# Decoder layer on one core: smaller last weight pieces, and a normalization step on GpSimd

## The chip, the cores and the metric

The kernel runs on one NeuronCore of a Trainium2 chip. The metric is the device time of one execution in microseconds, the median of several runs. A profile is one further execution; its span is the time from the first to the last event recorded on the core.

## The reference

One layer of a decoder trunk over 256 tokens of width 1024, all in float32. Two attention groups, a cross-attention and a mixture of 32 experts follow each other, each with a residual and a layer norm. The part that matters here is the last:

```python
def moe_ffn(h, w_router, b_router, w_mlp1, b_mlp1, w_mlp2, b_mlp2):
    ...
    y = jnp.zeros_like(xt)
    for e in range(N_EXPERTS):
        hid = clamped_swiglu(xt @ w_mlp1[e] + b_mlp1[e])
        y = y + combine[:, e:e + 1] * (hid @ w_mlp2[e] + b_mlp2[e])
    return y.reshape(B, S, D)
...
        ffn = moe_ffn(h, w_router[l], b_router[l], w_mlp1[l], b_mlp1[l], w_mlp2[l], b_mlp2[l])
        h = layer_norm(DEEPNORM_ALPHA * h + ffn, ln3_g[l], ln3_b[l])
```

Every token goes to 4 of the 32 experts. An expert has an up matrix of 1024 x 2048 (8 MB) and a down matrix of 1024 x 1024 (4 MB).

## The kernel before

**Stages.** The attention part takes the first fifth. Then the experts run one after another. For one expert TensorE gathers its up to 64 tokens (`gather`, L969), multiplies them with the up matrix (`up_stage`, L1059: 8 chunks `k` of 128 rows, 1 MB each, four products of 128x512 a chunk), VectorE and ScalarE form the clamped SwiGLU, TensorE turns it (`turn_hidden`, L1018) and multiplies with the down matrix (`down_stage`, L1097: two halves `u` of four chunks `c`, 0.5 MB and two products each), ScalarE copies the result (L1405), and TensorE scatters it into four banks (`scatter`, L981), which hold the sum for all tokens: banks 4 and 5 the two halves of the first 128 tokens, banks 6 and 7 those of the other 128. A product is two MATMUL instructions in the trace. Each expert's down stage runs behind the next expert's up stage, so that the order at the end is: up of 31, down of 30, down of 31, last scatter, final norm.

**Weights.** `ring` in SBUF has 24 places of 1 MB: two sets (parity) of two up pieces and one down piece, 4 MB each. SyncE issues all loads on one queue and waits ahead of each for the place to be free (`up_used`, `up_done`, `down_used`, `down_done`). In the loop a piece is one transfer. The last experts load halves of 2 MB, and the down pieces of experts 30 and 31 quarters of 1 MB (`load_quarter`, L558), each with a semaphore of its own: for the last, `last_half_in[0]`, `first_half_in`, `last_half_in[1]`, `piece_in`. TensorE waits for them ahead of chunk 0 and 2 of each half. The last expert's up piece comes in halves: chunks 6 and 7 wait for one transfer. Between the halves of the last down stage TensorE does the scatter of expert 30.

**Final norm.** The first 128 tokens: VectorE takes statistics from banks 4 and 5 (L1490 to L1494), GpSimd raises the variance to the power -0.5 (L599), and VectorE does two steps for each half of 512 columns: `(x - mean) * gain` out of the bank (L1500), then `x * rstd + bias` (L1504). The other 128: ScalarE sums (L1431) and sums squares (L1438) out of banks 6 and 7, GpSimd takes the power (L609), VectorE does the same two steps (L1911, L1914). ScalarE's passes write their elementwise output, which nobody reads, into `result[:, 1]`. SyncE sends each half to `out` as 256 KB (L580), when the semaphore `ln_ready` counts it, and waits for all four. The order on each engine is the order of the code.

## Time and profile before

| | us |
|---|---|
| median of 3 runs | 1140.28 |
| lowest and highest run | 1139.02, 1140.31 |
| the profiled execution | 1139.08 |
| its span | 1137.2 |
| TensorE matmul busy | 1090.2 (96%) |
| VectorE busy | 320.8 (28%) |
| ScalarE busy | 225.0 (20%) |
| GpSimd busy | 9.1 (1%) |

The span is 1.88 us shorter than the profiled execution's own time; the rest lies around it. TensorE's share is that of rows with pipelined ends. Times within the trace count from the span's start. The expert stage runs from about 230 us to 1128, the final norm from there to the end.

### The profile page before, as it was taken

What the parts mean: (1) busy time and instruction counts of PE and PEld (TensorE: products, weight loads), DVE (VectorE), ACT (ScalarE), POOL (GpSimd) and SP (SyncE); (2) the same over time, 40 slices, a digit from 0 to 9 for tenths busy, and PEclk for the clock granted to TensorE, in tenths of its full rate; (3) what the DMA queues carried; (4) which work ended last, traced back from release to release, by engine and by line L of the source; (5) the groups of instructions that cost most, each with busy time, mean ns of one, the idle gap of its engine ahead of it and who ended that gap; (6) DMA issues with size and microseconds to landing.
All of it is one profiled execution on the core that took longest, in us unless ns stands there. A gap on an engine that the chain in (4) does not pass through costs nothing.

```text
span 1137.2 us, 15690 instructions
## 1 busy us (share of the span) xinstructions
PE 1090.2 (96%) x6527; PEld 522.5 (46%) x6528; DVE 320.8 (28%) x727; ACT 225.0 (20%) x406; POOL 9.1 (1%) x14
## 2 busy tenths in 40 slices
PE   9999999999999999999999999999999999999996
PEld 6888899844333333334333333333333333334321
DVE  6987775552111111112111111111111111012113
ACT  5667565331000001001001000000000000001001
POOL 0000000000000000000000000000000000000000
PEclk9999999989999999999999999999999999999998
DMA  9856866699999999999999999999999999999996
GB/s 354 299 187 246 288 205 252 243 415 430 435 434 429 436 426 440 426 440 426 440 426 440 425 441 425 441 425 441 425 441 425 441 425 441 425 432 430 429 428 249
DMA packets 40144, 446.73 MB, mean 393 GB/s; under 512 B 4528, under 2 KB 5424, under 8 KB 24272
## 3 DMA queue, kind: packets, MB, share of 16 engines
q1 hardware_dynamic: 39824, 445.75, 93.5%
q10 hardware_dynamic: 288, 0.52, 0.1%
q8 instruction: 24, 0.39, 0.1%
q14 instruction: 8, 0.07, 0.0%
HBM read 445.21 MB, written 1.05 MB: 392 GB/s over the span
## 4 chain that ended last, share of the span: by engine, by line
PE 57%; DMA 38%; DVE 2%; SPq 1%; issue 1%; ACT 0%; DVEq 0%
DMA ring<-in_w_mlp 36%; PE bank L1059 24%; PE bank L1097 9%; PE bank L632 4%; PE bank L634 4%; PE bank L633 4%; PE bank L981 4%; PE bank L969 2%; DMA sub_g<-in_diff_subln_g 1%; PE bank L1018 1%; DMA w_raw<-in_w_in 1%; PE bank L873 1%; PE bank L857 1%; PE bank L1033 1%; SPq L465 0%
## 5 line engine op out<-in xcount | busy, mean ns | idle before, releaser
L1059 PE MATMUL bank<-ring,live 128*64 128x512 f32 x2048 | 471.2, 608 | 26.4 <-DMA ring<-in_w_mlp 25.8
L1059 PEld LDWEIGHTS bank<-ring,live 128*64 128x64 f32 x2048 | 144.2, 139 | 310.6 <-issue 290.8
L1097 PE MATMUL bank<-ring,live 128*64 128x512 f32 x992 | 220.4, 595 | 4.9 <-DMA ring<-in_w_mlp 4.9
L1796 DVE COPY live<-bank 128x256 f32<-128x256 f32 x32 | 13.6, 424 | 525.4 <-PE bank L1011 525.4
L1097 PEld LDWEIGHTS bank<-ring,live 128*64 128x64 f32 x992 | 68.7, 137 | 130.4 <-issue 122.0
L1401 ACT ACTIVATE live<-bank 128x512 f32<-128x512 f32 x31 | 18.5, 597 | 323.5 <-PE bank L1018 323.5
L1880 DVE TENSOR_SCALAR live<-bank 128x256 f32<-128x256 f32 x64 | 24.2, 420 | 199.0 <-PE bank L1059 199.0
L1473 DVE TENSOR_TENSOR w_low<-w_raw,w_high 128x1024 fp32r<-128x1024 f32 x61 | 72.0, 1222 | 14.5 <-ACT w_high L1186 14.2
L1397 ACT ACTIVATE live<-live 128x512 f32<-128x512 f32 x32 | 20.4, 636 | 246.2 <-DVE live L1880 246.2
L1186 ACT ACTIVATE w_high<-w_raw 128x1024 fp32r<-128x1024 f32 x61 | 62.8, 1059 | 28.6 <-DMA w_raw<-in_w_in 13.4
L969 PEld LDWEIGHTS bank<-pick,live 128*128 128x128 bf16 x1488 | 52.0, 118 | 25.2 <-issue 25.2
L632 PE MATMUL bank<-w_high,left 128*128 128x512 f32 x158 | 62.7, 397 | 0.5 <-DVE w_low L1473 0.2
L981 PE MATMUL bank<-live 64*128 64x512 f32 x248 | 61.6, 615 | 0.3 <-ACT live L1405 0.3
L634 PE MATMUL bank<-w_low,left 128*128 128x512 f32 x158 | 61.6, 390 | 0.0
L633 PE MATMUL bank<-w_high,left 128*128 128x512 f32 x158 | 61.6, 390 | 0.0
L1405 ACT ACTIVATE live<-bank 128x512 f32<-128x512 f32 x31 | 18.5, 597 | 203.6 <-PE bank L1097 203.6
L969 PE MATMUL bank<-pick,live 128*128 128x64 bf16 x1488 | 55.3, 198 | 0.0
L981 PEld LDWEIGHTS bank<-live 64*128 64x128 f32 x248 | 21.3, 186 | 41.0 <-issue 40.2
L632 PEld LDWEIGHTS bank<-w_high,left 128*128 128x128 f32 x158 | 29.7, 188 | 7.8 <-DVE w_low L1473 0.8
L634 PEld LDWEIGHTS bank<-w_low,left 128*128 128x128 f32 x158 | 29.6, 188 | 6.3
L633 PEld LDWEIGHTS bank<-w_high,left 128*128 128x128 f32 x158 | 29.7, 188 | 5.9
L1018 PEld LDWEIGHTS bank<-const,live 128*128 128x128 f32 x128 | 17.9, 210 | 26.0 <-issue 26.0
(233 smaller groups left out, 805.1 us busy)
## 6 DMA issues: line engine op xcount, KB each, us to landing
ring<-in_w_mlp SPq DMA_DIRECT2D x73, 4096.0 KB, 46.9
ring<-in_w_mlp SPq DMA_DIRECT2D x42, 2048.0 KB, 48.1
w_raw<-in_w_in SPq DMA_DIRECT2D x21, 512.0 KB, 8.8
w_raw<-in_w_mem_kv SPq DMA_DIRECT2D x16, 512.0 KB, 4.6
ring<-in_w_mlp SPq DMA_DIRECT2D x8, 1024.0 KB, 37.6
w_raw<-in_w_mix_out SPq DMA_DIRECT2D x8, 512.0 KB, 5.2
w_raw<-in_w_mem_q SPq DMA_DIRECT2D x8, 512.0 KB, 3.8
w_raw<-in_w_mem_o SPq DMA_DIRECT2D x8, 512.0 KB, 4.2
```

Of the source, the lines that this page charges most:

```text
L632: pe.matmul(out, stationary[0], moving[0], start=start, stop=False)
L633: pe.matmul(out, stationary[1], moving[0], start=False, stop=False)
L634: return pe.matmul(out, stationary[0], moving[1], start=False, stop=stop)
L969: mm = pe.matmul(xg[:, SLOTS * c:SLOTS * (c + 1)], h_parts[:, t, part, at:at + 4 * P - 3:4], pick[:, t, :], start=(n == 0), stop=(n == 5))
L981: mm = pe.matmul(acc[t][g][:, :], weights[rows, t, :], rows_out[rows, :], start=first, stop=last)
L1018: mm = pe.transpose(to[:, P * q:P * (q + 1)], glu[:, q:512:4], ident)
L1059: mm = pe.matmul(up[j][64 * g:64 * g + SLOTS, :], x_e[:, k, :], columns(row, j, g), start=False, stop=(k == KC - 1))
L1097: mm = pe.matmul(to[64 * g:64 * g + SLOTS, :], stationary[:, P * c + 64 * u:P * c + 64 * u + SLOTS], slot(at)[:, col:col + 512], start=(u ...
L1186: act.activation(w_high[:, (u + 2) % SPLIT], w_raw[:, u % RAW], ACT.Copy).then_inc(high_ready, 1)
L1397: act.activation(sig, glu, ACT.Sigmoid, scale=SW_ALPHA).then_inc(sig_ready, 1)
L1473: dve.tensor_tensor(w_low[:, u % RAW], w_raw[:, u % RAW], w_high[:, (u + 2) % SPLIT].bitcast(F32), ALU.subtract).then_inc(low_ready, 1)
L1880: last = dve.tensor_scalar(glu[:, S * n:S * (n + 1)], hid[:, :, 0], LIMIT, None, ALU.min)
```

## The change

**Pieces.** The second half of the last expert's second up piece is loaded as two transfers of 1 MB, and TensorE waits for each ahead of chunks 6 and 7 (`last_up_in`, then `piece_in`). Of the last down piece the first and the last quarter are loaded as two eighths of 0.5 MB each; TensorE waits for them ahead of chunks 0, 1 and 6, 7. That makes three more transfers (one up, two down).

**Norm.** VectorE centres both halves of the first 128 tokens, `(x - mean) * gain`, and counts them in `last_centred`. GpSimd then multiplies with `rstd` and adds the bias, as two instructions for each half (`stretch_last`): the first half ahead of the power for the other 128 tokens, the second behind it. VectorE centres both halves of the other 128 tokens, each behind a wait for ScalarE's sum of squares of that half, and then does both second steps. ScalarE's elementwise outputs go to `unused_out`, a place of the ring that is no longer needed. The outputs of the first 128 tokens wait for `first_out`, those of the others for `ln_ready`.

```diff
@@ -247,6 +247,7 @@
         last_y = at_place("last_y", [P, 512], F32, 4, 2048)
         last_back = at_place("last_back", [P, NT, P], F32, 4, 4096)
         result = at_place("result", [P, NT, D], F32, 1)
+        unused_out = at_place("unused_out", [P, 2, 512], F32, 6)
         mean_parts, square_sums = stats[:, 1, 0, 0:3], stats[:, 1, 1, 0:3]
 
         filled_to = {}
@@ -473,14 +477,23 @@
                         sp.wait_ge(up_used, before * 3 + 2)
                     load(e, k, 3 * parity + k)
 
-            def load_up_halves(e, before, parity):
+            def load_part(e, k, at, of, count, landed):
+
+                part = slice(8192 * of // count, 8192 * (of + 1) // count)
+                sp.dma_start(slot(at)[:, part], expert_src(e, k)[:, part]).then_inc(landed, 16)
+
+            def load_up_halves(e, before, parity, last=False):
 
                 for n in range(2 * UPS):
                     if n < 3:
                         sp.wait_ge(up_used, before * 3 + n + 1)
                     else:
                         sp.wait_ge(up_done, before + 1)
-                    load_half(e, n // 2, 3 * parity + n // 2, n % 2)
+                    if last and n == 3:
+                        load_part(e, 1, 3 * parity + 1, 2, 4, last_up_in)
+                        load_part(e, 1, 3 * parity + 1, 3, 4, piece_in[3 * parity + 1])
+                    else:
+                        load_half(e, n // 2, 3 * parity + n // 2, n % 2)
 
             def load_down(e, before, parity):
 
@@ -557,7 +570,7 @@
                 part = slice(2048 * quarter, 2048 * (quarter + 1))
                 sp.dma_start(slot(at)[:, part], expert_src(e, UPS)[:, part]).then_inc(landed, 16)
 
-            load_up_halves(E - 1, sp.snap(more * E + (E - 3)), 1)
+            load_up_halves(E - 1, sp.snap(more * E + (E - 3)), 1, last=True)
             sp.wait_ge(down_used, sp.snap(more * E + (E - 3)))
             load_quarter(E - 2, UPS, 0, before_last_half_in[0])
             load_quarter(E - 2, UPS, 1, first_half_in[UPS])
@@ -565,20 +578,24 @@
             load_quarter(E - 2, UPS, 2, before_last_half_in[1])
             load_quarter(E - 2, UPS, 3, piece_in[UPS])
             sp.wait_ge(down_used, sp.snap(more * E + (E - 2)))
-            load_quarter(E - 1, 3 + UPS, 0, last_half_in[0])
+            load_part(E - 1, UPS, 3 + UPS, 0, 8, last_eighth_in[0])
+            load_part(E - 1, UPS, 3 + UPS, 1, 8, last_half_in[0])
             load_quarter(E - 1, 3 + UPS, 1, first_half_in[3 + UPS])
             sp.wait_ge(down_done, sp.snap(more * E + (E - 2)))
             load_quarter(E - 1, 3 + UPS, 2, last_half_in[1])
-            load_quarter(E - 1, 3 + UPS, 3, piece_in[3 + UPS])
+            load_part(E - 1, UPS, 3 + UPS, 6, 8, last_eighth_in[1])
+            load_part(E - 1, UPS, 3 + UPS, 7, 8, piece_in[3 + UPS])
 
             sp.wait_ge(up_done, sp.snap(sweeps * E))
             for i, name in enumerate(("ln3_g", "ln3_b")):
                 sp.dma_start(last_gb[:, i, :], row(a[name])).then_inc(last_gb_in, 16)
-            for t in range(NT):
-                for q in range(2):
-                    sp.wait_ge(ln_ready, 12 + 2 * t + q + 1)
-                    sp.dma_start(a["out"][0, P * t:P * (t + 1), 512 * q:512 * (q + 1)],
-                                 result[:, t, 512 * q:512 * (q + 1)]).then_inc(out_written, 16)
+            for t, q in ((0, 0), (0, 1), (1, 0), (1, 1)):
+                if t:
+                    sp.wait_ge(ln_ready, 12 + q + 1)
+                else:
+                    sp.wait_ge(first_out, q + 1)
+                sp.dma_start(a["out"][0, P * t:P * (t + 1), 512 * q:512 * (q + 1)],
+                             result[:, t, 512 * q:512 * (q + 1)]).then_inc(out_written, 16)
             sp.wait_ge(out_written, 16 * 2 * NT)
 
 
@@ -605,8 +622,19 @@
             pool.tensor_tensor(rms[:, 2, :], rms[:, 1, :], half.broadcast_to([P, 8]), ALU.pow).then_inc(rms_rstd, 1)
             for n in range(2, 7):
                 inverse_root(n)
+
+            def stretch_last(q):
+                x = result[:, 0, 512 * q:512 * (q + 1)]
+                pool.wait_ge(last_centred, q + 1)
+                pool.wait_ge(rstd_ready, 7)
+                pool.tensor_scalar(x, x, ln_s[:, 6, 1:2], None, ALU.mult).then_inc(last_scaled, 1)
+                pool.wait_ge(last_scaled, q + 1)
+                pool.tensor_tensor(x, x, last_gb[:, 1, 512 * q:512 * (q + 1)], ALU.add).then_inc(first_out, 1)
+
+            stretch_last(0)
             pool.wait_ge(last_var_ready, 1)
             pool.tensor_tensor(ln_s[:, 7, 1:2], ln_s[:, 7, 0:1], half, ALU.pow).then_inc(rstd_ready, 1)
+            stretch_last(1)
 
 
         @block.tensor
@@ -1022,7 +1050,7 @@
 
                 return rows[:, 1024 * j:1024 * (j + 1)].rearrange("p (m a n) -> p m a n", a=2, n=8)[:, :, g, :]
 
-            def up_stage(n, at, loads, first_loads=None, earlier=None, first=False, first_sum=False, weights=False, bias=False, tokens=False, scatter_first=False):
+            def up_stage(n, at, loads, first_loads=None, earlier=None, first=False, first_sum=False, weights=False, bias=False, tokens=False, scatter_first=False, seventh=None):
 
 
 
@@ -1049,8 +1077,12 @@
                 for k in range(KC):
                     if k % 4 == 0 and first_loads:
                         pe.wait_ge(first_half_in[at + k // 4], first_loads)
-                    if k % 4 == (2 if first_loads else 0):
+                    if k == KC - 2 and seventh is not None:
+                        pe.wait_ge(seventh, 16)
+                    elif k % 4 == (2 if first_loads else 0):
                         pe.wait_ge(piece_in[at + k // 4], loads)
+                    if k == KC - 1 and seventh is not None:
+                        pe.wait_ge(piece_in[at + 1], loads)
                     if first and k == 4:
                         pe.wait_ge(x_e_ready, 1)
                     for j in range(2):
@@ -1079,15 +1111,17 @@
                 pe.wait_ge(back_ready, n)
                 gather()
 
-            def down_stage(n, at, loads, to, first_loads=None, stationary=hidT, between=None, halves=(None, None)):
+            def down_stage(n, at, loads, to, first_loads=None, stationary=hidT, between=None, halves=(None, None), eighths=None):
 
 
                 pe.wait_ge(hidT_ready, n)
                 for u in range(2):
                     for c in range(4):
-                        if c == 0 and halves[u] is not None:
+                        if eighths is not None and 4 * u + c in (0, KC - 2):
+                            pe.wait_ge(eighths[u], 16)
+                        if c == (1 if eighths is not None and u == 0 else 0) and halves[u] is not None:
                             pe.wait_ge(halves[u], 16)
-                        if c == (0 if halves[u] is None else 2):
+                        if c == (0 if halves[u] is None else 3 if eighths is not None and u else 2):
                             if first_loads and u == 0:
                                 pe.wait_ge(first_half_in[at], first_loads)
                             else:
@@ -1138,7 +1172,7 @@
             up_stage(of_end[1], ups[0], loads, 64, earlier=(of_end[3], of_end[2]))
             gather_next(of_end[1])
             down_stage(of_end[2], downs[1], pe.snap(loads - 16), ty, 48)
-            up_stage(of_end[0], ups[1], loads, 64, earlier=(of_end[2], of_end[1]), scatter_first=True)
+            up_stage(of_end[0], ups[1], loads, 64, earlier=(of_end[2], of_end[1]), scatter_first=True, seventh=last_up_in)
             pe.wait_ge(back_ready, of_end[0])
             turn_picks(of_end[0])
             down_stage(of_end[1], downs[0], loads, ty, 48, between=lambda: turn_hidden(of_end[0], up[0]),
@@ -1149,7 +1183,8 @@
                 pe.wait_ge(back_ready, of_end[0])
                 scatter()
 
-            down_stage(of_end[0], downs[1], loads, up[1], 64, last_hidT, between=scatter_before, halves=last_half_in)
+            down_stage(of_end[0], downs[1], loads, up[1], 64, last_hidT, between=scatter_before, halves=last_half_in,
+                       eighths=last_eighth_in)
             pe.wait_ge(y_ready, of_end[0])
             pe.wait_ge(back_ready, pe.snap(more * E + (E + 1)))
             scatter(last=True)
@@ -1428,14 +1463,14 @@
             copy_result(end, banks[1][:, :], last_y[:, :])
             for q in range(2):
                 act.wait_ge(all_added, 2 + q + 1)
-                act.activation(result[:, 1, 512 * q:512 * (q + 1)], banks[6 + q][:, :], ACT.Copy, scale=-1.0 / D,
+                act.activation(unused_out[:, q, :], banks[6 + q][:, :], ACT.Copy, scale=-1.0 / D,
                                accum_out=mean_parts[:, q:q + 1]).then_inc(tail_sums, 1)
             act.wait_ge(tail_sums, 2)
             act.activation(mean_parts[:, 2:3], mean_parts[:, 0:1], ACT.Identity, bias=mean_parts[:, 1:2])\
                 .then_inc(minus_mean_ready, 1)
             act.wait_ge(minus_mean_ready, 1)
             for q in range(2):
-                act.activation(result[:, 1, 512 * q:512 * (q + 1)], banks[6 + q][:, :], ACT.Square, bias=mean_parts[:, 2:3],
+                act.activation(unused_out[:, q, :], banks[6 + q][:, :], ACT.Square, bias=mean_parts[:, 2:3],
                                accum_out=square_sums[:, q:q + 1]).then_inc(tail_sums, 1)
                 if q == 0:
                     act.wait_ge(tail_sums, 3)
@@ -1903,13 +1938,19 @@
             step(last)
             variance(6)
             dve.wait_ge(last_gb_in, 32)
-            apply_norm(6, result[:, 0, :], [banks[4 + q][:, :] for q in range(2)], last_gb)
-            dve.wait_ge(minus_mean_ready, 1)
-            dve.wait_ge(last_var_ready, 1)
             for q in range(2):
                 half_row = slice(512 * q, 512 * (q + 1))
-                step(dve.scalar_tensor_tensor(out=result[:, 1, half_row], in0=banks[6 + q][:, :], scalar=mean_parts[:, 2:3],
-                                              in1=last_gb[:, 0, half_row], op0=ALU.add, op1=ALU.mult))
+                dve.scalar_tensor_tensor(out=result[:, 0, half_row], in0=banks[4 + q][:, :], scalar=mv_ln[:, 6, 0:1],
+                                         in1=last_gb[:, 0, half_row], op0=ALU.subtract, op1=ALU.mult).then_inc(last_centred, 1)
+            dve.wait_ge(minus_mean_ready, 1)
+            for q in range(2):
+                half_row = slice(512 * q, 512 * (q + 1))
+                dve.wait_ge(tail_sums, 3 + 2 * q)
+                dve.scalar_tensor_tensor(out=result[:, 1, half_row], in0=banks[6 + q][:, :], scalar=mean_parts[:, 2:3],
+                                         in1=last_gb[:, 0, half_row], op0=ALU.add, op1=ALU.mult).then_inc(second_mean, 1)
+            for q in range(2):
+                half_row = slice(512 * q, 512 * (q + 1))
+                dve.wait_ge(second_mean, q + 1)
                 dve.wait_ge(rstd_ready, 8)
                 dve.scalar_tensor_tensor(out=result[:, 1, half_row], in0=result[:, 1, half_row], scalar=ln_s[:, 7, 1:2],
                                          in1=last_gb[:, 1, half_row], op0=ALU.mult, op1=ALU.add).then_inc(ln_ready, 1)
```

How the instructions stand on the engines (the tag in brackets is the semaphore waited for). TensorE in the last down stage (`last_hidT` is the last expert's hidden product), before:

```order
L1097 MATMUL bank<-ring,last_hidT 64x512 [waits last_half_in0,hidT_ready]
L1097 MATMUL bank<-ring,last_hidT 64x512 x3
L1097 MATMUL bank<-ring,last_hidT 64x512 [waits first_half_in5]
L1097 MATMUL bank<-ring,last_hidT 64x512 x3
L981 MATMUL bank<-live 128x512 [waits back_ready,y_ready]
L981 MATMUL bank<-live 128x512 x3
L1097 MATMUL bank<-ring,last_hidT 64x512 [waits last_half_in1]
L1097 MATMUL bank<-ring,last_hidT 64x512 x3
L1097 MATMUL bank<-ring,last_hidT 64x512 [waits piece_in5]
L1097 MATMUL bank<-ring,last_hidT 64x512 x3
```

and after:

```order
L1131 MATMUL bank<-ring,last_hidT 64x512 [waits last_eighth_in0,hidT_ready]
L1131 MATMUL bank<-ring,last_hidT 64x512
L1131 MATMUL bank<-ring,last_hidT 64x512 [waits last_half_in0]
L1131 MATMUL bank<-ring,last_hidT 64x512
L1131 MATMUL bank<-ring,last_hidT 64x512 [waits first_half_in5]
L1131 MATMUL bank<-ring,last_hidT 64x512 x3
L1009 MATMUL bank<-live 128x512 [waits back_ready,y_ready]
L1009 MATMUL bank<-live 128x512 x3
L1131 MATMUL bank<-ring,last_hidT 64x512 [waits last_half_in1]
L1131 MATMUL bank<-ring,last_hidT 64x512 x3
L1131 MATMUL bank<-ring,last_hidT 64x512 [waits last_eighth_in1]
L1131 MATMUL bank<-ring,last_hidT 64x512
```

The last pair waits for `piece_in5`. No product has moved; two waits are added, and the scatter stays between the halves.

VectorE's final norm behind the variance, before (`last_gb` holds gain and bias, `stats` the mean of the other 128 tokens, `ln_s` the powers):

```order
L1500 SCALAR_TENSOR_TENSOR result<-bank,mv_ln,last_gb 128x512 [waits last_gb_in]
L1504 SCALAR_TENSOR_TENSOR result<-result,ln_s,last_gb 128x512 [waits rstd_ready,dve_step]
L1500 SCALAR_TENSOR_TENSOR result<-bank,mv_ln,last_gb 128x512
L1504 SCALAR_TENSOR_TENSOR result<-result,ln_s,last_gb 128x512 [waits dve_step]
L1911 SCALAR_TENSOR_TENSOR result<-bank,stats,last_gb 128x512 [waits last_var_ready,minus_mean_ready]
L1914 SCALAR_TENSOR_TENSOR result<-result,ln_s,last_gb 128x512 [waits rstd_ready,dve_step]
L1911 SCALAR_TENSOR_TENSOR result<-bank,stats,last_gb 128x512
L1914 SCALAR_TENSOR_TENSOR result<-result,ln_s,last_gb 128x512 [waits rstd_ready,dve_step]
```

and after:

```order
L1943 SCALAR_TENSOR_TENSOR result<-bank,mv_ln,last_gb 128x512 [waits last_gb_in]
L1943 SCALAR_TENSOR_TENSOR result<-bank,mv_ln,last_gb 128x512
L1949 SCALAR_TENSOR_TENSOR result<-bank,stats,last_gb 128x512 [waits tail_sums,minus_mean_ready]
L1949 SCALAR_TENSOR_TENSOR result<-bank,stats,last_gb 128x512 [waits tail_sums]
L1955 SCALAR_TENSOR_TENSOR result<-result,ln_s,last_gb 128x512 [waits rstd_ready,second_mean] x2
```

Two of the eight instructions have left the engine, and GpSimd, which before had only the powers, has this in its last rows:

```order
L616 TENSOR_TENSOR ln_s<-ln_s,small 128x1 [waits var_ready] x5
L630 TENSOR_SCALAR result<-result,ln_s 128x512 [waits rstd_ready,last_centred]
L632 TENSOR_TENSOR result<-result,last_gb 128x512 [waits last_scaled]
L636 TENSOR_TENSOR ln_s<-ln_s,small 128x1 [waits last_var_ready]
L630 TENSOR_SCALAR result<-result,ln_s 128x512 [waits rstd_ready,last_centred]
L632 TENSOR_TENSOR result<-result,last_gb 128x512 [waits last_scaled]
```

The second power (L636) now stands behind the first multiply and add.

## Rows read from the trace of the kernel before

**Rows 1.** The page's 40 slices of the span: GB/s that the DMA engines moved.
```profile
GB/s 354 299 187 246 288 205 252 243 415 430 435 434 429 436 426 440 426 440 426 440 426 440 425 441 425 441 425 441 425 441 425 441 425 441 425 432 430 429 428 249
```
**Rows 2.** The chain of waits, its end: start us, us, what.
```profile
1083.32 34.49 DMA ring<-in_w_mlp
...
1117.85 1.94 PE bank L1097 x8
...
1134.05 0.75 DVE result L1914
```
**Rows 3.** Timeline of PE and its weight loads: start us, us, instruction, idle before.
```profile
1103.18 3.65 PE L1059 MATMUL bank<-ring,live 128*64 128x512 f32 x16 [1.25 <-DMA ring<-in_w_mlp]
...
1112.99 0.32 PEld L1097 LDWEIGHTS bank<-ring,live 128*64 128x64 f32 x4 [0.54 <-DMA ring<-in_w_mlp]
1115.52 1.94 PE L1097 MATMUL bank<-ring,last_hidT 128*64 128x512 f32 x8 [0.47 <-DMA ring<-in_w_mlp]
...
1121.64 3.65 PE L1097 MATMUL bank<-ring,last_hidT 128*64 128x512 f32 x16
```
**Rows 4.** Line L558, last expert: its first two quarters, then its last two.
```profile
L558 SPq DMA_DIRECT2D ring<-in_w_mlp x2: 328/381/434, 1082.9 to 1083.3; - x2
...
DMA to landing us min/median/max: 32.4/33.5/34.5
...
L558 SPq DMA_DIRECT2D ring<-in_w_mlp x2: 4214/5456/6699, 1087.4 to 1094.2; - x2
...
DMA to landing us min/median/max: 28.6/30.7/32.8
```
**Rows 5.** DMA view of the first 28 us: GB/s in 40 slices, packets.
```profile
GB/s 0 0 47 126 277 258 234 291 281 354 404 401 407 410 401 406 399 400 423 424 421 421 395 410 404 404 415 424 433 410 430 383 407 416 402 402 422 383 395 404
DMA packets 4943, 9.89 MB, mean 353 GB/s; under 512 B 412, under 2 KB 924, under 8 KB 4942
```
**Rows 6.** Timeline of the final norm: VectorE (DVE), GpSimd (POOL), ScalarE (ACT).
```profile
1128.79 0.15 DVE L1494 TENSOR_SCALAR ln_s<-mv_ln 128x1 f32<-128x1 f32 x1
1128.86 0.74 DVE L1500 SCALAR_TENSOR_TENSOR result<-bank,mv_ln,last_gb 128x512 f32<-128x512 f32 x1
1129.02 0.55 POOL L599 TENSOR_TENSOR ln_s<-ln_s,small 128x1 f32<-128x1 f32 x1 [898.40 <-DVE ln_s L1494]
1129.68 0.75 DVE L1504 SCALAR_TENSOR_TENSOR result<-result,ln_s,last_gb 128x512 f32<-128x512 f32 x1
...
1130.29 0.19 ACT L1438 ACTIVATION_READ_ACCUMULATOR result<-bank,stats 128x1 f32 x1
1130.35 0.74 DVE L1500 SCALAR_TENSOR_TENSOR result<-bank,mv_ln,last_gb 128x512 f32<-128x512 f32 x1
...
1131.19 0.19 ACT L1438 ACTIVATION_READ_ACCUMULATOR result<-bank,stats 128x1 f32 x1
...
1131.79 0.55 POOL L609 TENSOR_TENSOR ln_s<-ln_s,small 128x1 f32<-128x1 f32 x1 [2.21 <-ACT ln_s L1445]
```
**Rows 7.** Timeline, GpSimd's earlier powers and what VectorE ran beside them.
```profile
19.76 2.35 DVE L1473 TENSOR_TENSOR w_low<-w_raw,w_high 128x1024 fp32r<-128x1024 f32 x2
19.92 1.46 POOL L599 TENSOR_TENSOR ln_s<-ln_s,small 128x1 f32<-128x1 f32 x1 [1.00 <-DVE ln_s L1494]
...
97.07 1.65 POOL L605 TENSOR_TENSOR turned_weights<-turned_weights,small 128x8 f32<-128x8 f32 x1 [75.69 <-DVE turned_weights L1713]
...
137.03 0.74 DVE L1500 SCALAR_TENSOR_TENSOR h<-h,mv_ln,gb 128x512 f32<-128x512 f32 x1
137.20 0.98 POOL L599 TENSOR_TENSOR ln_s<-ln_s,small 128x1 f32<-128x1 f32 x1 [38.48 <-DVE ln_s L1494]
```
**Rows 8.** Line L580, outputs; then a stretch's busy times, PEclk, DMA share, GB/s.
```profile
L580 SPq DMA_DIRECT2D out<-result x4: 332/334/343, 1130.5 to 1134.8; - x4
...
DMA to landing us min/median/max: 2.0/2.0/2.0
...
1130.30:1132.40 2.10, 0.00 (x0) 0.00 (x0) 2.06 (x4) 1.34 (x6) 0.55 (x1) 0.50 0.32 125
```

3 lines of the change are left out of this document (added).

## Prediction

> **What bounds the kernel now.** I read the slices of the page first, then the chain of waits, then the timeline of the last 40 us engine by engine. The slices [rows 1] show 415 to 441 GB/s from the ninth to the last but one, with no gap: from there on the kernel takes expert weights as fast as they come. The chain [rows 2] says the same of the end: one stretch of weight transfer runs up to 1117.81, and only behind it do compute engines set the time. So an edit counts only if it makes the second quarter of the last down piece land earlier, or shortens what follows: TensorE from 1117.85 to 1125.3, the copy and last scatter to 1128.05, the final norm on VectorE to 1134.80, the last output transfer and the end at 1137.2. What has room ahead of 1117.85 is no gain unless it moves that landing.
>
> **Part 1: smaller pieces.** What TensorE does with them, step by step.
> *Last up piece.* Before, chunks 6 and 7 of the last expert wait for one 2 MB transfer; TensorE idles 1.25 us in front of 1103.18 and then runs both in 3.65 us, to 1106.83 [rows 3]. Now chunk 6 waits for its own 1 MB. It lands about 2.4 us earlier (1.05 MB at 430 GB/s, [rows 1]), near 1100.8, while TensorE is still busy until 1103.18 - 1.25 = 1101.93. So the 1.25 us go and the up stage ends near 1105.6. What is late next: the down stage of expert 30, whose four quarters arrive about 2.4 us apart, each with 8 MATMULs, half of 3.65, so 1.83 us of work. It ends 0.47 ahead of 1115.52 now, at 1115.05 [rows 3]; by the same arrivals it would end no earlier than 1112.99, where the weight loads wait for the fourth quarter [rows 3], plus 1.83, which is 1114.8. Of the 1.25 us some 0.2 is left, and the next wait takes that: the last down stage starts at 1115.52 for its first quarter, and its third and fourth chunks at 1117.85 for the second [rows 2, 3].
> *First eighths.* Chunk 0 can start near 1114.8 rather than 1115.5, but chunks 2 and 3 still wait for the second quarter, issued at 1083.3 and landed 34.5 us later, at 1117.8 [rows 4]. The bytes ahead of it in the queue are the same. Gain 0.
> *Last eighths.* The fourth quarter was issued at 1094.2 and landed 28.6 us later, at 1122.8 [rows 4]. TensorE starts the second half of that stage at 1121.64 and comes to chunk 6 after 8 of its 16 instructions, 1121.64 + 1.83 = 1123.47 [rows 3]. The data has been there for 0.67 us. Gain 0, as long as that cover lasts; if the fourth quarter came over 0.67 us later, the eighths would save at most the rest, up to 0.9 us.
> *Cost.* Three more transfers are issued on SyncE, at 0.33 to 0.43 us where the queue takes them at once [rows 4], with over 28 us of queue behind: nothing. The eighths move 4 KB rows. The nearest rows for small packets are the first 28 us, where all but one are under 8 KB: once full, the slices there move 383 to 433 GB/s [rows 5], about 405, against 430. For the 1.05 MB of eighths ahead of the second quarter that is 2.59 - 2.44 = 0.15 us at worst, at best 0. The quarters of 8 KB rows landed 2.4 us apart, so they cost nothing. I take 0. The gains of ScalarE and VectorE (hidden product 1.25 us earlier) end in the same waits. The two rows of the last gain and bias are issued when the up stage is done, 1.2 us earlier, behind all weights in the queue.
> **Part 1 is worth 0**, from -0.9 to +0.15.
>
> **Part 2: the final norm.** Before, VectorE runs eight instructions of 0.74 to 0.75 us behind the variance, from 1128.86 to 1134.80 [rows 2, 6]. Now two of them, the second steps of the first 128 tokens, go to GpSimd as four: multiply and add for each half, in line with the two powers. VectorE keeps six. Centring both halves has no wait in between, start 0.67 apart as other rows do: 1128.86 to 1130.27. The centring of the other 128 tokens waits for ScalarE's first sum of squares, 1130.48, and the second, 1131.38 [rows 6]: 1130.56 to 1131.30 and 1131.46 to 1132.2. The last two steps wait for the power, which ended at 1132.34 [rows 6]. If GpSimd cost nothing VectorE would end at 1132.45 + 0.67 + 0.75 = 1133.87, 0.93 earlier. But the outputs now leave in the order (0,0), (0,1), (1,0), (1,1) on one queue, and (0,1) comes from GpSimd's last add, so both later ones stand behind it.
>
> *GpSimd's price.* It has no row of 128x512. From below: VectorE's 0.75 for the same shape [rows 6], so 1.50 a pair. From above: its power of 8 elements took 1.65, of one 0.55 [rows 7], 0.157 per element; at that rate a half row takes 80 us. A power is far from a multiply, and I give that end no more than a few in a hundred and leave it outside the range. Between them I add to VectorE's 0.75 what GpSimd's one-element row costs above VectorE's of 0.15 (L1494 [rows 6]), 0.40: 1.15 for the add with two inputs. For the multiply with one input I take 0.95. Pair: 2.10; for the range up to 3.0, twice VectorE's rows.
> [...]
>
> *The queue.* Power of token half 0 to 1129.57; multiply from 1129.68 (the first centring ends 1129.60) to 1130.63; 0.10 for the wait; add to 1131.88. The second power stands behind that: it starts at 1131.91, not 1131.79. So 0.12 is lost there, and it ends at 1132.46. Then multiply and add of the second half.
>
> *The port.* The earlier powers [rows 7] show what happens when the two engines meet. A power of one element takes 0.55 beside a VectorE row that reads a bank (1129.02 [rows 6]). Beside an instruction with two inputs in SBUF it takes as long as that lasts and 0.41 to 0.45 more: started 137.20, the other ended 137.77, it ended 138.18; started 19.92, the other (1.18 each) ended 20.93, it ended 21.38. So only one of them has the interface, and it is given back between two VectorE instructions. The last steps on VectorE have both inputs in SBUF. I take it that it holds both ways. GpSimd's second multiply starts right behind its own power, 1132.49 to 1133.44; VectorE, which needs 0.11 to hear of the power, stands behind it: 1133.44 to 1134.14. Then GpSimd's add, 1134.14 to 1135.29, and VectorE's last step, to 1135.99.
> The Trainium skill, SBUF — State Buffer, section "SBUF: two separate sides", states this as an exclusive lock held for the whole instruction, by a VectorE instruction with two SBUF inputs against a GpSimd one that reads SBUF, whoever starts first. The powers [rows 7] agree with it in one direction; the other no run here shows yet.
>
> *The outputs.* A 256 KB output lands 2.0 us after its issue, issues take 0.34, and one keeps the DMA engines 0.32 x 2.1 = 0.67 us [rows 8]. Before they were 1.1 us and more apart. Now three go in a row: issues at 1135.34, 1135.68, 1136.03. The third lands at 1136.03 + 2.0 at the earliest, but the three transfers need 1135.34 + 1.33 + 3 x 0.67 = 1138.67. Before, the last landed at 1134.83 + 2.0 = 1136.83, 0.37 before the end. **Part 2 costs** 1138.67 + 0.37 - 1137.2 = 1.84, say 1.9 us.
>
> **Sum.** The profiled execution took 1139.08, 1.88 more than its span, and lies 1.20 under the median of 1140.28. I put 1.9 on the median: 1142.2.
>
> **Rivals.**
> *A, no blocking* (the port is shared when GpSimd comes first). Then add at 1133.54 to 1134.69, issue 1134.74, landed 1138.07, end 1138.44: +1.2, 1141.5. For it: no row of before has GpSimd ahead of VectorE. Against: the three stretched powers.
> *C, VectorE first at the port*, which ends on the slower side. Both start within 0.1 us of the power's end. If VectorE gets in first: step 1132.57 to 1133.32, multiply to 1134.27, last step to 1134.97, add to 1136.12, three issues from 1136.17, end 1139.87: +2.7, 1143.0, 0.24% above before. It decides from the point where GpSimd takes more than 0.1 us from its power to its next read. For it: after the port came free the power took 0.41 of its 0.55, so some 0.14 lies ahead of its read.
> *D, GpSimd dearer than 2.3 us a pair.* Each 0.1 us on a pair counts twice, once before the second power, once behind. At 2.5 case B (the forecast) gives +2.7, at 3.0 it gives +3.7, 1144.0.
> *E, cheap GpSimd or late weights.* At 1.5 a pair, without blocking and with outputs that overlap in the DMA engines, the last issue is at 1134.7, -0.1; in executions where the fourth quarter comes late, the eighths take back up to 0.9. 1139.4 to 1140.7. For it: the runs of before spread over 1.3 us, and the profile is one of the fast ones.
> *F, the pieces don't do what they say*: the second quarter is the wait that counts and stays whole. That is in the forecast already.
>
> **How the numbers follow.** About 0.2% (2.3 us) is what a measurement of this kernel can tell from no change. Forecast 0.33, A 0.24, C 0.15, D 0.12, E 0.16. Range: from 1139.8, inside E, to 1144.0, the upper end of D. Slower by over 0.2% is above 1142.6: C 0.12, D 0.12 and 0.08 of the forecast's own spread, 0.32. Faster is below 1138.0, deep in E: 0.04. The rest, 0.64, is the same.
>
> **What would show it.** Right: TensorE's last up rows without the 1.25 us gap, and the third chunk of the last down stage still at about 1117.8; GpSimd's multiply and add near 0.95 and 1.15; VectorE's first last step twice as long as 0.75 or late; the second power near 1131.9; three outputs issued 0.34 apart, the last landing more than 2.0 after its issue. Wrong: a landing of the second quarter that moves by over 0.3 us, a multiply or add over 1.3, VectorE's last steps of 0.75 beside a GpSimd row (then A), or an end of VectorE before 1134.

## The result, and the profile after

The changed kernel takes 1143.21 us in the median of its runs, against 1140.31 for the kernel before: a ratio of 1.0025, 95% interval 1.0017 to 1.0033, or 2.9 us slower. Its profiled execution took 1141.85, with a span of 1140.1 (before 1139.08 and 1137.2). Of eleven executions of each kernel one was far off, at 2222.55 before and 4011.12 after, and the ratio leaves both out. The result is inside the range of the prediction and 1.0 us above the point; at 0.25% slower it lies beyond the 0.2% to which the prediction drew "the same".

TensorE behind the last up stage, from the timeline of the changed kernel (start us, us, instruction, idle before it and what ended it):

```profile
1098.28 7.09 PE L1091 MATMUL bank<-ring,live 128*64 128x512 f32 x32 [0.23 <-DMA ring<-in_w_mlp]
...
1105.73 1.94 PE L1131 MATMUL bank<-ring,live 128*64 128x512 f32 x8
1108.08 1.94 PE L1131 MATMUL bank<-ring,live 128*64 128x512 f32 x8 [0.41 <-DMA ring<-in_w_mlp]
...
1114.80 1.89 PE L1131 MATMUL bank<-ring,last_hidT 128*64 128x512 f32 x8
...
1118.00 1.94 PE L1131 MATMUL bank<-ring,last_hidT 128*64 128x512 f32 x8 [1.31 <-DMA ring<-in_w_mlp]
...
1126.21 1.99 PE L1009 MATMUL bank<-last_y,last_back 64*128 64x512 f32 x8 [0.77 <-ACT last_y L1440]
```

The same third chunk in the timeline of the kernel before:

```profile
1117.85 1.94 PE L1097 MATMUL bank<-ring,last_hidT 128*64 128x512 f32 x8 [0.39 <-DMA ring<-in_w_mlp]
```

The gap of 1.25 us inside the last up stage [rows 3] is gone: 32 instructions run in one piece. Two waits for weights take its place: 0.41 us in expert 30's down stage, which had none there, and in front of the third chunk of the last down stage 1.31 us instead of 0.39. That chunk starts at 1118.00, 0.15 later than before. From there to the last scatter it is 8.21 us in both.

The final norm, same view, VectorE (DVE), GpSimd (POOL) and SyncE's queue:

```profile
1129.01 1.40 DVE L1943 SCALAR_TENSOR_TENSOR result<-bank,mv_ln,last_gb 128x512 f32<-128x512 f32 x2
...
1129.90 1.57 POOL L630 TENSOR_SCALAR result<-result,ln_s 128x512 f32<-128x512 f32 x1 [0.18 <-DVE result L1943]
...
1130.73 1.58 DVE L1949 SCALAR_TENSOR_TENSOR result<-bank,stats,last_gb 128x512 f32<-128x512 f32 x2 [0.32 <-ACT unused_out L1473]
...
1131.56 1.27 POOL L632 TENSOR_TENSOR result<-result,last_gb 128x512 f32<-128x512 f32 x1
1132.78 0.57 POOL L636 TENSOR_TENSOR ln_s<-ln_s,small 128x1 f32<-128x1 f32 x1
1132.85 4.84 SPq L597 DMA_DIRECT2D out<-result  x4
1133.34 1.57 POOL L630 TENSOR_SCALAR result<-result,ln_s 128x512 f32<-128x512 f32 x1
1133.46 1.77 DVE L1955 SCALAR_TENSOR_TENSOR result<-result,ln_s,last_gb 128x512 f32<-128x512 f32 x2 [1.15 <-POOL ln_s L636]
1134.99 1.36 POOL L632 TENSOR_TENSOR result<-result,last_gb 128x512 f32<-128x512 f32 x1
```

VectorE's two last steps by line (count: duration ns min/median/max, first and last start us; shapes):

```profile
L1955 DVE SCALAR_TENSOR_TENSOR result<-result,ln_s,last_gb x2: 737/924/1111, 1133.5 to 1134.5; 128x512 f32<-128x512 f32 x2
```

GpSimd's multiply takes 1.57 us, its add 1.27 and 1.36. The second power starts at 1132.78 instead of 1131.79 [rows 6]. VectorE ends at 1135.23, GpSimd at 1136.35, where VectorE alone ended at 1134.80. The outputs, by the line of their issues, from 1136.7 on (the third and fourth):

```profile
L597 SPq DMA_DIRECT2D out<-result x2: 431/446/461, 1136.8 to 1137.2; - x2
...
DMA to landing us min/median/max: 2.3/2.3/2.4
```

The last one is issued at 1137.2 instead of 1134.8, and lands 2.4 us later instead of 2.0 [rows 8].

**How the traces are compared.** The weights run up to 3 us earlier or later from one execution to the next, long before anything that was changed. So each trace is read in three stretches: W, from chunk 4 of the last up stage to the third chunk of the last down stage (the weights); T, from there to the last scatter (TensorE); N, from there to the span's end (the norm). The spans are given to 0.1 us, so an N is good to 0.05 and a difference of two to 0.1. e4, e5, e6, e8, e9 and e10 ran once each, for their traces.

| kernel | W | T | N |
|---|---|---|---|
| before | 19.58 | 8.21 | 11.14 |
| changed | 19.72 | 8.21 | 13.89 |
| e1, pieces alone | 19.72 | 8.21 | 11.16 |
| e2, norm alone | 19.53 | 8.21 | 13.86 |
| e3, other order of outputs | 19.72 | 8.21 | 12.53 |
| e4, multiply with two inputs | 19.71 | 8.21 | 12.94 |
| e5, last steps from the bank | 19.67 | 8.21 | 13.76 |
| e6, one half on GpSimd | 19.58 | 9.03 | 11.78 |
| e7, VectorE alone | 19.48 | 8.21 | 10.60 |
| e8, up quarters only | 19.58 | 8.21 | 11.19 |
| e9, eighths only | 19.62 | 8.21 | 11.15 |
| e10, multiply by a constant | 19.57 | 8.21 | 13.71 |

N grew by 2.75 us, W by 0.14. That is the 2.9. (In e11 and e12 the scatter has moved, so they have no W and T of this kind and stand below.)

### The profile page after: what moved, and what is told of

It reads as the page before. It is cut to its first block, busy times and chain, and to the rows that moved or that the text cites. A ratio compares the mean times of both kernels' runs of the same rounds, so it can differ in the third digit from the quotient of the medians.

```text
span 1140.1 us, 15697 instructions
## 1 busy us (share of the span) xinstructions
PE 1089.1 (96%) x6528; PEld 524.0 (46%) x6528; DVE 319.5 (28%) x725; ACT 225.2 (20%) x406; POOL 14.9 (1%) x18
## 4 chain that ended last, share of the span: by engine, by line
PE 57%; DMA 37%; SPq 2%; DVE 1%; issue 0%; ACT 0%; POOL 0%; POOLq 0%; another core or an unknown queue 0%
DMA ring<-in_w_mlp 36%; PE bank L1091 23%; PE bank L1131 9%; PE bank L660 5%; PE bank L662 5%; PE bank L661 5%; PE bank L1009 4%; PE bank L997 2%; DMA w_raw<-in_w_in 2%; SPq L483 1%; PE bank L1046 1%; PE bank L901 1%; PE bank L885 1%; SPq L469 1%; PE bank L1061 1%
## 5 line engine op out<-in xcount | busy, mean ns | idle before, releaser
L1091 PE MATMUL bank<-ring,live 128*64 128x512 f32 x2048 | 470.1, 607 | 24.4 <-DMA ring<-in_w_mlp 23.8
```

The costliest lines, as they stand in the source:

```text
L1091: mm = pe.matmul(up[j][64 * g:64 * g + SLOTS, :], x_e[:, k, :], columns(row, j, g), start=False, stop=(k == KC - 1))
```

## The experiments

My theory behind the trace: all but 0.15 us is GpSimd's, by the length of its four instructions, by the place of the second power behind two of them, and by outputs that stand behind its last add. The rivals: the pieces slow the weights; the new order of VectorE's steps loses by itself; GpSimd is slow only because the port is contended.

### The two parts apart (e1, e2)

e1 is the diff without its norm hunks, e2 the diff without its piece hunks.

> The change's first part alone: the last up piece in quarters and the eighths, with the final norm of the kernel before. My theory (the pieces move no landing that counts, all of the loss is GpSimd's) expects 0.0 us against the kernel before, 0.3 at most, with the third chunk of the last down stage near 1117.9 us and an idle gap of some 1.3 us ahead of it. The rival (smaller packets or fewer bytes in the queue slow the weights) expects the 0.14 us by which that chunk was later in the changed kernel, or more in executions other than the profiled one: up to 1.5 of the 2.9 us here.

> The change's second part alone: the norm step on GpSimd, with the weight pieces of the kernel before. My theory expects the whole loss, +2.7 to +2.9 us, with GpSimd's multiply at 1.57 us and its add at 1.27 to 1.36, the second power at about 1132.6, and the last issue of an output near 1137.1. The rival expects 1.4 to 2.5.

e1 measured 1140.63 in the median against 1140.43, ratio 1.0006 (0.9997 to 1.0015); e2 1142.74, ratio 1.0019 (1.0010 to 1.0028). These repeated runs alone leave the pieces between -0.3 and +1.7 us. They put e2 2.3 us above the kernel before (1.1 to 3.2), less than the 2.7 to 2.9 expected and inside the rival's 1.4 to 2.5, so they do not decide between the two. The stretches are sharper. e1 has N = 11.16, as before, and W = 19.72; e2 has all of the loss in N, 13.86, and W = 19.53. The timeline of e1 shows the gap in front of the third chunk, with the norm as it was:

```profile
1114.13 1.89 PE L1117 MATMUL bank<-ring,last_hidT 128*64 128x512 f32 x8
1117.33 1.94 PE L1117 MATMUL bank<-ring,last_hidT 128*64 128x512 f32 x8 [1.31 <-DMA ring<-in_w_mlp]
```

So the loss in N is the norm's, and what the pieces gained in the up stage ended in this wait.

### Which of the pieces costs (e8, e9)

e8 keeps the two quarters of the last up half and drops the eighths; e9 the reverse.

> Only the last up half in two transfers, nothing else of the change. From the start of chunk 4 of the last expert's up stage to that of the third chunk of its last down stage it took 19.58 us before and 19.72 with all pieces. If the 4 KB rows of the eighths cost that, 19.58 here, and TensorE runs its last 32 up instructions without the gap of 1.25 us; if it is the number of transfers or the up quarters, 19.65 to 19.72.

> Only the eighths of the last down piece, with the last up half whole. If the 4 KB rows cost the 0.14 us, the stretch from chunk 4 of the last up stage to the third chunk of the last down stage takes 19.72 us here; otherwise 19.6. The 1.2 us gap in front of the last 16 up instructions is back. The stretch from that third chunk to the last scatter stays 8.21 us, with or without eighths.

W was 19.58 in e8 and 19.62 in e9. The six traces with all pieces (changed, e1, e3, e4, e5, e10) have 19.57 to 19.72, mean 19.69, the four with the pieces of before (before, e2, e6, e7) 19.48 to 19.58, mean 19.54. The pieces cost about 0.14 us together. Which of them, and whether it is the rows of 4 KB or the number of transfers, stays open: e8 came out as it should if the 4 KB rows cost it, but e9, which has them, came out at 19.6 as it should if they do not, and both lie within the spread of the others.

### The order of the outputs (e3)

```diff
-            for t, q in ((0, 0), (0, 1), (1, 0), (1, 1)):
+            for t, q in ((0, 0), (1, 0), (1, 1), (0, 1)):
```

> The changed kernel with one edit: the outputs leave in the order (0,0), (1,0), (1,1), (0,1), so that the two of VectorE do not stand behind GpSimd's last one. Theory: in the changed kernel the last three issues were bunched behind the end of the last add (1136.35), and the last one landed 2.4 us after its issue instead of 2.0. With this order the last issue is at 1136.4 and lands at 1138.4: 1.1 to 1.3 us less than the changed kernel, so +1.7 us against before. If the end of GpSimd's work alone set the time and the transfers overlapped, it would be 0 to 0.4 us less.

e3 measured 1141.67 in the median, ratio 1.0010 (1.0001 to 1.0019), 1.2 us above the kernel before where 1.7 was expected. N fell by 1.36 us to 12.53. The last output left right behind GpSimd's add, which ended at 1138.61, and landed 2.0 us later. The add in the timeline of e3

```profile
1137.25 1.36 POOL L632 TENSOR_TENSOR result<-result,last_gb 128x512 f32<-128x512 f32 x1
```

and by line of the issue:

```profile
L597 SPq DMA_DIRECT2D out<-result x1: 332/332/332, 1138.6 to 1138.6; - x1
...
DMA to landing us min/median/max: 2.0/2.0/2.0
```

So about half of the loss in N was outputs queued behind the slowest one: two issues (0.8 us), 0.4 of landing in a bunch, and some 0.1 between the last landing and the end.

### What GpSimd's multiply costs (e4, e10)

e4 reads the deviation as a row of equal elements, e10 multiplies by a constant:

```diff
-                pool.tensor_scalar(x, x, ln_s[:, 6, 1:2], None, ALU.mult)
+                pool.tensor_tensor(x, x, ln_s[:, 6, 1:2].broadcast_to([P, 512]), ALU.mult)
```

```diff
-                pool.tensor_scalar(x, x, ln_s[:, 6, 1:2], None, ALU.mult)
+                pool.tensor_scalar(x, x, 0.5, None, ALU.mult)
```

> The changed kernel with GpSimd's multiply as an instruction with two tensor inputs (the reciprocal deviation read as a row of 512 equal elements) instead of one with a scalar. If GpSimd's time goes with the number of inputs, it takes as long as the multiply or longer, 1.57 us or more. If the form with a scalar is the slow one, it takes 1.27 us as the add, and the pair 2.54 instead of 2.84; as each pair stands once before and once behind the second power, the end moves by 0.6 us.

> The changed kernel with GpSimd's multiply by the constant 0.5 in the instruction instead of the column of reciprocal deviations, so that the first 128 tokens are not scaled by their own. The multiply took 1.57 us with the column and 1.04 us as a two-input instruction. If the column operand makes it slow, it takes 1.1 us or less here, and VectorE's delay beside it (0.37) goes or shrinks; if this kind of instruction is slow whatever its scalar, it stays at 1.57.

From the timeline of e4:

```profile
1132.86 0.55 POOL L636 TENSOR_TENSOR ln_s<-ln_s,small 128x1 f32<-128x1 f32 x1
1133.37 1.04 POOL L630 TENSOR_TENSOR result<-result,ln_s 128x512 f32<-128x512 f32 x1
1133.51 1.45 DVE L1955 SCALAR_TENSOR_TENSOR result<-result,ln_s,last_gb 128x512 f32<-128x512 f32 x1 [0.55 <-POOL ln_s L636]
...
1134.49 1.59 POOL L632 TENSOR_TENSOR result<-result,last_gb 128x512 f32<-128x512 f32 x1
...
1134.88 1.75 DVE L1955 SCALAR_TENSOR_TENSOR result<-result,ln_s,last_gb 128x512 f32<-128x512 f32 x1
```

and of e10:

```profile
1135.32 1.50 POOL L630 TENSOR_SCALAR result<-result 128x512 f32<-128x512 f32 x1
```

with VectorE's two last steps beside it, by line:

```profile
L1955 DVE SCALAR_TENSOR_TENSOR result<-result,ln_s,last_gb x2: 737/882/1027, 1135.4 to 1136.4; 128x512 f32<-128x512 f32 x2
```

The form with a scalar is the slow one: 1.57 us with a column, 1.50 with a constant, against 1.04 with two inputs. So the column operand is not what makes it slow; what does is not shown. VectorE's delay beside it shrank from 0.37 to 0.29 us in e10. e4's pair took 2.31 instead of 2.84. Its second power started 6.00 us behind the last scatter's start, against 6.57 in the changed kernel and 5.73 before: the pair is what holds the power back. N fell by 0.95, more than the 0.6 expected of it, since the multiply took 1.04 and not 1.27. Two multiplies of 0.53 less would be 1.06, but behind the second power the add took 1.59 us instead of 1.36, and VectorE lost more to the port too (below).

### The port (e5, e6)

e5 lets VectorE's two last steps read the bank:

```diff
-                dve.scalar_tensor_tensor(out=result[:, 1, half_row], in0=result[:, 1, half_row], scalar=ln_s[:, 7, 1:2],
+                dve.scalar_tensor_tensor(out=result[:, 1, half_row], in0=banks[6 + q][:, :], scalar=ln_s[:, 7, 1:2],
```

> The changed kernel, with VectorE's two last steps reading the bank instead of the centred row, so that they have one input in SBUF and leave the centring out of what they use. In the changed kernel the first of them took 1.11 us beside GpSimd's multiply and GpSimd's second add 1.36 us. If that is the shared SBUF interface, here both steps take 0.75, back to back, and the add 1.27 us. If it is something else (a late start, GpSimd slow by itself at that place), 1.11 and 1.36 stay. From the start of the last scatter to the end of the span 13.8 us, against 13.89 in the changed kernel.

The timeline of e5:

```profile
1135.37 1.57 POOL L630 TENSOR_SCALAR result<-result,ln_s 128x512 f32<-128x512 f32 x1
1135.49 1.41 DVE L1955 SCALAR_TENSOR_TENSOR result<-bank,ln_s,last_gb 128x512 f32<-128x512 f32 x2 [1.14 <-POOL ln_s L636]
...
1137.02 1.26 POOL L632 TENSOR_TENSOR result<-result,last_gb 128x512 f32<-128x512 f32 x1
```

As the port would have it: the two steps take 0.75 each, back to back, and the add 1.26. So the 1.11 and 1.36 of the changed kernel are contention for SBUF; it is worth about 0.1 us in N, and the 1.57 of the multiply is its own.

e6 leaves one half to GpSimd, with the power between its two instructions, on the pieces of before. VectorE does the second step of the other half ahead of its centring of the other tokens, and the outputs leave in the order (0,1), (1,0), (0,0), (1,1). GpSimd's part:

```diff
+            x = result[:, 0, 0:512]
+            pool.tensor_scalar(x, x, ln_s[:, 6, 1:2], None, ALU.mult).then_inc(last_scaled, 1)
             pool.wait_ge(last_var_ready, 1)
             pool.tensor_tensor(ln_s[:, 7, 1:2], ln_s[:, 7, 0:1], half, ALU.pow).then_inc(rstd_ready, 1)
+            pool.wait_ge(last_scaled, 1)
+            pool.tensor_tensor(x, x, last_gb[:, 1, 0:512], ALU.add).then_inc(first_out, 1)
```

> GpSimd keeps one half only: on the pieces of the kernel before, GpSimd multiplies and adds the first half of the first 128 tokens, with the second power between the two, and VectorE does the other seven steps. From the rows so far, counted from the start of the last scatter: multiply 3.7 to 5.3, power undisturbed at 5.7 to 6.3, add from 6.3 with two inputs in SBUF. If the port is held by a two-input instruction of GpSimd for its whole length, VectorE's first last step is held until 7.6 and the last one ends near 8.9, later than the 8.74 of the kernel before and the 8.17 of VectorE alone: 11.2 to 11.4 us to the end. If it is held for a part only, as beside the multiply (0.37), the last step ends near 8.2 to 8.4: 10.7 to 10.9 us.

The timeline of e6:

```profile
1130.21 1.57 POOL L619 TENSOR_SCALAR result<-result,ln_s 128x512 f32<-128x512 f32 x1 [0.18 <-DVE result L1922]
1130.75 0.75 DVE L1926 SCALAR_TENSOR_TENSOR result<-result,ln_s,last_gb 128x512 f32<-128x512 f32 x1
...
1132.24 0.57 POOL L621 TENSOR_TENSOR ln_s<-ln_s,small 128x1 f32<-128x1 f32 x1 [0.46 <-ACT ln_s L1459]
1132.78 1.26 POOL L623 TENSOR_TENSOR result<-result,last_gb 128x512 f32<-128x512 f32 x1
1132.92 2.34 DVE L1938 SCALAR_TENSOR_TENSOR result<-result,ln_s,last_gb 128x512 f32<-128x512 f32 x2
```

and its two last steps by line:

```profile
L1938 DVE SCALAR_TENSOR_TENSOR result<-result,ln_s,last_gb x2: 740/1207/1674, 1132.9 to 1134.5; 128x512 f32<-128x512 f32 x2
```

VectorE's step beside the two-input add took 1.67 us: 1132.92 to 1134.59, that is until the add ended at 1134.04, and 0.55. In e4 the same: 1.45 until 0.55 behind the multiply's end, 1.75 until 0.55 behind the add's. GpSimd is held as well when VectorE is first. In the changed kernel the second add started 0.24 us before VectorE's step ended and took 0.09 more than 1.27; in e4 it started 0.47 before the end and took 0.32 more; in e5, beside nothing, it took 1.26. That is the overlap less 0.15 each time, near the 0.14 that the prediction put ahead of GpSimd's read.

The first two rows of e6 show more of the multiply with one input. VectorE's step at L1926 also has two inputs in SBUF; it started 0.54 us behind the start of the multiply and took 0.75, with no delay. In the changed kernel VectorE's step started 0.12 behind the multiply and lost 0.37, as if held until 0.49 behind its start; in e10 until 0.41. So the multiply seems to hold the port at its beginning only, not for its 1.57 us. This is worked out from three rows and was not tested by itself.

In e6 the last step ended 8.74 us behind the scatter's start, exactly as before the change. Three outputs then left in a bunch, and N was 11.78, worse than the 11.14 of before and than the 11.2 to 11.4 I expected. A side finding in T: here, with the pieces of before, the fourth quarter of the last down piece came late, a wait of 0.59 us in TensorE's timeline:

```profile
1123.81 1.94 PE L1111 MATMUL bank<-ring,last_hidT 128*64 128x512 f32 x8 [0.59 <-DMA ring<-in_w_mlp]
```

T grew to 9.03. It is the case in which the last eighths have something to save; of the twelve traces of the table it is the only one.

### VectorE alone (e7)

The norm hunks with GpSimd's `stretch_last` taken out and this in front of the centring of the other tokens:

```diff
+            dve.wait_ge(rstd_ready, 7)
+            for q in range(2):
+                half_row = slice(512 * q, 512 * (q + 1))
+                dve.wait_ge(last_centred, q + 1)
+                dve.scalar_tensor_tensor(out=result[:, 0, half_row], in0=result[:, 0, half_row], scalar=ln_s[:, 6, 1:2],
+                                         in1=last_gb[:, 1, half_row], op0=ALU.mult, op1=ALU.add).then_inc(first_out, 1)
```

> The norm without GpSimd's four instructions, with the weight pieces of the kernel before: VectorE does all eight steps, in the changed kernel's order (both centrings, both second steps, both centrings of the other tokens, both second steps). Theory: the loss is GpSimd's and not that of the new order; the order alone saves VectorE the waits between dependent steps, 8 x 0.67 instead of 5.94 us, so the last step ends 0.4 to 0.5 us earlier against the start of the last scatter: 10.7 us from there to the end, against 11.14 before. In the whole time that is -0.4 us, which the rounds can hardly tell from 0. Rival: the waits for the sums of squares or a port conflict with the second power put the last step as late as before or later, 11.1 us or more.

VectorE in e7's timeline:

```profile
1130.51 1.40 DVE L1915 SCALAR_TENSOR_TENSOR result<-bank,mv_ln,last_gb 128x512 f32<-128x512 f32 x2
...
1131.82 1.41 DVE L1921 SCALAR_TENSOR_TENSOR result<-result,ln_s,last_gb 128x512 f32<-128x512 f32 x2
...
1133.14 1.41 DVE L1927 SCALAR_TENSOR_TENSOR result<-bank,stats,last_gb 128x512 f32<-128x512 f32 x2
...
1134.46 1.41 DVE L1933 SCALAR_TENSOR_TENSOR result<-result,ln_s,last_gb 128x512 f32<-128x512 f32 x2
```

Eight steps in 5.36 us instead of 5.94, N = 10.60, 0.54 less than before and 3.3 less than with GpSimd. The order loses nothing; it gains. The repeated runs give 1139.70 against 1140.33, ratio 0.9999 (0.9990 to 1.0008): the gain is too small for them, and rests on N.

### A version that uses the pieces (e11, e12)

TensorE's 1.31 us of waiting has to be filled with work that otherwise comes later. The scatter of expert 30 moves from between the halves to behind the second chunk, with the norm of e7:

```diff
+                        if eighths is not None and u == 0 and c == 1:
+                            between()
...
-                    if u == 0 and between:
+                    if u == 0 and between and eighths is None:
```

e12 is the same with the pieces of before.

> A version meant to use the pieces: the changed kernel's pieces, the norm on VectorE alone, and the scatter of expert 30 moved from between the halves of the last down stage to behind its second chunk, where TensorE waits 1.31 us for the second quarter in the changed kernel. From the rows: chunks 0 and 1 end at 1116.7 on the clock of the changed kernel's trace, scatter to 1118.6, chunks 2 and 3 to 1120.5, the second half 3.65 us more, to 1124.2 instead of 1125.46, if the fourth quarter is there by 1123.3. From chunk 4 of the last up stage to the start of the last scatter 26.7 us instead of 27.93 (before: 27.79), and 10.6 from there to the end instead of 11.14: 1.6 to 1.8 us under the kernel before in all. If the fourth quarter's landing decides, half a microsecond of it is lost; if ScalarE's copy of expert 30's result is late, more.

> The same with the pieces of the kernel before, so it differs from the last one by the pieces alone. The first two chunks start at 1115.5 on the clock of the trace of before and end at 1117.4, scatter to 1119.3, chunks 2 and 3 to 1121.2, the second half to 1124.8: 27.3 us from chunk 4 of the last up stage to the last scatter, 0.5 less than before, and 10.6 to the end. If the pieces are worth something once TensorE has work for the gap, this one is 0.6 us slower than the last; if their 0.14 to 0.18 us of later landing and nothing else counts, it is not slower.

e11 took 1138.56 against 1139.99: ratio 0.9984, 0.9975 to 0.9993. e12 1139.18, ratio 0.9989, 0.9980 to 0.9998. Both are faster than the kernel before, e12 barely clear of noise, and so faster than the changed one. TensorE in e11:

```profile
1099.90 7.09 PE L1081 MATMUL bank<-ring,live 128*64 128x512 f32 x32 [0.23 <-DMA ring<-in_w_mlp]
...
1116.33 1.89 PE L1121 MATMUL bank<-ring,last_hidT 128*64 128x512 f32 x8
1118.14 1.99 PE L999 MATMUL bank<-live 64*128 64x512 f32 x8
1120.06 5.55 PE L1121 MATMUL bank<-ring,last_hidT 128*64 128x512 f32 x24
1126.39 1.99 PE L999 MATMUL bank<-last_y,last_back 64*128 64x512 f32 x8 [0.77 <-ACT last_y L1432]
```

and in e12:

```profile
1099.73 3.65 PE L1066 MATMUL bank<-ring,live 128*64 128x512 f32 x16 [0.32 <-DMA ring<-in_w_mlp]
...
1126.83 1.99 PE L988 MATMUL bank<-last_y,last_back 64*128 64x512 f32 x8 [0.77 <-ACT last_y L1414]
```

No wait for weights is left in the last down stage of e11. From chunk 4 of the last up stage to the last scatter it is 26.49 us in e11 (1099.90 to 1126.39) and 27.10 in e12 (1099.73 to 1126.83), 27.79 before; N is 10.61 and 10.57. By the traces e11 gains 1.8 us on the kernel before and e12 1.3, by the medians 1.4 and 0.8; about 0.5 of each is the norm of e7. With the scatter in the gap the pieces are worth 0.6 us; their two ratios overlap, so this rests on one trace of each.

## Why the prediction was right or wrong

**Part 1, right.** The gap in the up stage went, the up stage ended at 1105.4 (forecast 1105.6), the first chunks of the last down stage started at 1114.80 (1114.8), and the next waits took it all, the one for the second quarter most. I took 0 for the cost of the pieces and bounded it by 0.15; about 0.14 it was. That bound came from rows of 4 KB, and e8 and e9 do not show that these are the cause, so the agreement is in part luck.

**Part 2, the mechanisms right, one term mis-sized.** The term is GpSimd's price of a pair: 2.10 in the sum, 2.84 measured. The multiply is what was off, 1.57 against the 0.95 taken; the add was 1.27 against 1.15. I had made the one-input instruction the cheaper one, and on GpSimd this form is the dearer. One of the prediction's own signs of being wrong, a multiply over 1.3, was met. The Trainium skill, GPSIMD Engine Reference, section 3.1, gives 769 ns for 512 elements of a tight loop; that is half of the 1.57 us that the rows show for this instruction. That the pair counts twice, once ahead of the second power, was right: the power started at 1132.78 on the trace's clock, where the forecast had 1131.91.

**The port, half right.** The forecast had VectorE's first last step wait for the end of GpSimd's multiply, and GpSimd's add for the end of that step. With the one-input multiply VectorE lost 0.37 us, not the rest of the multiply; it was done at 1134.57, before the multiply ended at 1134.91, and the add was not held back by 0.60. With two-input instructions (e4, e6) it holds VectorE as forecast: VectorE is done 0.55 behind GpSimd's end (forecast 0.70). The Trainium skill, SBUF — State Buffer, section "SBUF: two separate sides", has the port locked for the whole of a GpSimd instruction. e4 and e6 agree, with VectorE done 0.55 us behind GpSimd's end; the multiply with one input does not: VectorE was done 0.34 us before it ended, and in e6 a step beside its later part was not delayed.

**The outputs, right in kind.** Three left in a row, and the last landed late, 2.4 us behind its issue where I had 2.64. e3 shows that this order, which the prediction named, was worth 1.36 us.

**The sum.** With the pair at 2.84 the prediction's own formula (each 0.1 counts twice) gives 1.84 + 1.48 = 3.3; less the 0.60 by which the add was not held, 2.7, against 2.75 measured in N. The rival "GpSimd dearer than 2.3 us a pair" is what happened, with the mild port of rival A. Rival C, VectorE first at the port, did not: in every trace GpSimd's next instruction started right behind its power and 0.1 us ahead of VectorE's. The point was 1.0 us low; the range held, and it was slower, as forecast. That it was not further off is partly luck: the dear multiply (+1.48) and the milder port (-0.60) are two errors of opposite sign. Rival D had a chance of 0.12, and "slower by over 0.2%", where the result fell, 0.32 against 0.64 for the same, so the chances leaned to the wrong side.

## What to carry to other kernels

Taking work off a busy engine at the end pays only if the engine that takes it is done by then, with everything queued behind it: four instructions on GpSimd took 5.8 us where VectorE's two had needed 1.5. Before splitting a transfer, ask which wait behind it comes next, and move work into that wait along with it: the pieces were worth -0.1 us by themselves and about +0.6 with the scatter in the gap. And put the slowest output last in its queue.

## What the runs showed of the hardware

- GpSimd in float32, 128x512 in place: multiply by a column 1.57 us, by a constant 1.50, product of two inputs with one of them a repeated column 1.04, add of two full inputs 1.26 to 1.27. Whether 1.04 and 1.27 differ by the operation or by the repeated column is not shown. VectorE's fused step on the same shape takes 0.75.
- A GpSimd instruction with two SBUF inputs keeps a VectorE instruction with two SBUF inputs out until its end, and VectorE's then needs 0.55 us more (e4 twice, e6 once). With VectorE first, GpSimd's is held for the overlap less 0.15 us (the changed kernel, e4). The multiply with one input, 1.57 us long, delayed a VectorE step that started 0.12 us behind it by 0.37, and one that started 0.54 behind it not at all (e6). A VectorE instruction that reads a bank is not delayed: 0.75 us each in e5.
- Three outputs of 256 KB issued in a row landed 2.0, 2.3 and 2.4 us behind their issue, and the issues themselves grew from 0.34 to 0.46 us.
- With all the pieces the issue of the second eighth took 10.81 us, so the second quarter was issued at 1094.2, not 1083.3, and 23.8 us ahead of its landing instead of 34.5. With the eighths alone (e9) the two took 0.81 us to issue, and it was the second quarter's own issue, begun at 1084.47, that took 10.30. So the eighths by themselves do not hold the queue; what does is not shown. The later issue cost at most the 0.14 us in W. SyncE's issues in the changed kernel:

```profile
1083.33 10.81 SPq L483 DMA_DIRECT2D ring<-in_w_mlp  x1
1094.18 2.69 SPq L571 DMA_DIRECT2D ring<-in_w_mlp  x1
```

and in e9:

```profile
1083.62 0.81 SPq L482 DMA_DIRECT2D ring<-in_w_mlp  x2
1084.47 10.30 SPq L567 DMA_DIRECT2D ring<-in_w_mlp  x1
```
